# Launch order, pooling means on ScalarE, two row buffers for thirteen pairs of weight sums, and channel tiles added ahead of their sums

## What is computed

```python
    c_act = jax.nn.silu(c)
    mod = (c_act @ w_ada[l] + b_ada[l])[:, None, :]
    u = layer_norm(x) * (1 + sc_m) + sh_m
    z = u @ w_in[l]
    y_pool = pool_mixer(z_pool, w_pool[l], pool_scale[l]) @ w_br_pool[l]
    y_attn = chunk_attention(z_q, z_k, z_v, rel_bias[l]) @ w_br_attn[l]
    y_conv = conv_module(z_conv, conv_w[l], conv_b[l], conv_ln_g[l], conv_ln_b[l]) @ w_br_conv[l]
    merged = gates[:, :, 0] * y_pool + gates[:, :, 1] * y_attn + gates[:, :, 2] * y_conv
    x = layer_norm(ALPHA * x + g_m * (merged @ w_o[l]), ln_mix_g[l], ln_mix_b[l])
    h = jnp.square(jax.nn.relu(u @ w_ff1[l] + b_ff1[l]))        # u from the new x
    x = layer_norm(ALPHA * x + g_f * (h @ w_ff2[l] + b_ff2[l]), ln_ff_g[l], ln_ff_b[l])
```

## Time and profile before

| what | value |
|---|---|
| median of 3 runs | 1504.99 us (1504.74 to 1505.49) |
| the profiled execution | 1508.53 us, span 1506.4 us |
| TensorE busy | 1445.0 us, 96% |
| VectorE busy | 980.5 us, 65% |
| ScalarE busy | 586.4 us, 39% |
| GpSimd busy | 474.5 us, 31% |
| mean granted clock of TensorE | 0.992 of full speed |

### The profile page before, as it was taken

How to read it: one execution, slowest core, us unless ns; L and a number is a source line. 1 busy time by engine, 2 the same in 40 slices (tenths; PEclk the granted TensorE clock), 3 DMA queues, 4 the chain that set the end, 5 groups by cost and what they waited for, 6 DMA issues and landing times.

```text
span 1506.4 us, 17601 instructions
## 1 busy us (share of the span) xinstructions
PE 1445.0 (96%) x6802; PEld 1203.4 (80%) x6802; DVE 980.5 (65%) x1244; ACT 586.4 (39%) x824; POOL 474.5 (31%) x385
## 2 busy tenths in 40 slices
PE   7799899999899999997999999999999999999998
PEld 7687688878778888886888887788888888888886
DVE  3878697878867445432376879766565644675494
ACT  3311254544554111110252766444444544433351
POOL 1007500000000788996202534344344311240021
PEclk9999999999999999998999999999999999999999
DMA  9774110000102667766362264444443869656371
GB/s 351 239 252 128 41 30 23 29 28 23 29 1 62 225 236 267 270 252 214 119 215 92 84 234 157 140 154 154 154 154 133 277 233 362 225 182 230 120 236 57
DMA packets 149124, 241.51 MB, mean 160 GB/s; under 512 B 9464, under 2 KB 79278, under 8 KB 147000
## 3 DMA queue, kind: packets, MB, share of 16 engines
q1 hardware_dynamic: 134824, 177.04, 35.2%
q0 software_dynamic: 14224, 63.45, 11.3%
HBM read 170.17 MB, written 70.29 MB: 160 GB/s over the span
## 4 chain that ended last, share of the span: by engine, by line
PE 67%; DVE 11%; DMA 8%; POOL 7%; issue 3%; ACT 3%; SPq 0%; DVEq 0%; ACTq 0%; POOLq 0%
PE ps L1878 19%; PE ps L1880 18%; PE ps L1879 18%; PE ps L1979 7%; DMA tw_scratch<-tw_sum 6%; PE ps L1898 2%; POOL tw_sum L780 2%; POOL tw_rows L781 1%; PE ps L2037 1%; DVE partial L1341 1%; POOL tw_sum L783 1%; POOL tw_sum L778 1%; DVE bn L1308 1%; DVE mid L1624 1%; DVE mid L1427 1%
## 5 line engine op out<-in xcount | busy, mean ns | idle before, releaser
L1878 PE MATMUL ps<-act_hi,w_hi 128*128 128x512 f32 (+1 forms) x512 | 199.9, 390 | 9.4 <-DVE w_lo L1498 8.8
L1879 PE MATMUL ps<-act_lo,w_hi 128*128 128x512 f32 (+1 forms) x512 | 196.9, 385 | 0.0
L1880 PE MATMUL ps<-act_hi,w_lo 128*128 128x512 f32 (+1 forms) x512 | 196.8, 384 | 0.0
L1745 DVE TENSOR_TENSOR part_lo<-k_raw,part_hi 128x1024 fp32r<-128x1024 f32 x112 | 154.2, 1414 | 49.0 <-ACT part_hi L866 46.7
L1878 PE MATMUL ps<-part_hi 128*128 128x512 f32 x448 | 174.3, 389 | 0.0
L1879 PE MATMUL ps<-part_lo,part_hi 128*128 128x512 f32 x448 | 174.3, 389 | 0.0
L1880 PE MATMUL ps<-part_hi,part_lo 128*128 128x512 f32 x448 | 174.3, 389 | 0.0
L866 ACT ACTIVATE part_hi<-k_raw 128x1024 fp32r<-128x1024 f32 x112 | 116.3, 1059 | 110.2 <-DMA k_raw<-tw_scratch 84.3
L1498 DVE TENSOR_TENSOR w_lo<-w_raw,w_hi 128x1024 fp32r<-128x1024 f32 x30 | 63.7, 2122 | 116.3 <-ACT w_hi L866 116.3
L1878 PEld LDWEIGHTS ps<-act_hi,w_hi 128*128 128x128 f32 x512 | 97.0, 189 | 30.1 <-DVE w_lo L1498 9.7
L1879 PEld LDWEIGHTS ps<-act_lo,w_hi 128*128 128x128 f32 x512 | 97.0, 190 | 19.1 <-issue 0.7
(11 more groups left out here) (250 smaller groups left out, 3403.9 us busy)
## 6 DMA issues: line engine op xcount, KB each, us to landing
k_raw<-h_scratch SPq DMA_DIRECT2D x112, 256.0 KB, 4.0
k_raw<-tw_scratch SPq DMA_DIRECT2D x112, 256.0 KB, 5.3
ada<-in_w_ada_dram SPq DMA_DIRECT2D x11, 2048.0 KB, 10.1
w_raw<-in_w_in_dram SPq DMA_DIRECT2D x42, 512.0 KB, 5.2
tw_rows<-in_w_ff_dram POOLq DMA_DIRECT2D x16, 1024.0 KB, 5.5
tw_scratch<-tw_rows POOLq DMA_DIRECT2D x16, 1024.0 KB, 4.3
h_scratch<-h_sum POOLq DMA_DIRECT2D x64, 256.0 KB, 3.2
pair_raw<-in_w_ff_dram SPq DMA_DIRECT2D x13, 1024.0 KB, 6.0
```

The source lines that it names most:

```text
L1745: nc.vector.tensor_tensor(part_lo[s][:, :, :], k_raw[rs][:, :, :], f(part_hi[s][:, :, :]), ALU.subtract)\
L1878: nc.tensor.matmul(out, sh, mh, start=first, stop=False)
L1879: nc.tensor.matmul(out, sh, ml, start=False, stop=False)
L1880: return nc.tensor.matmul(out, sl, mh, start=False, stop=last)
```

## The change

- Launch: TensorE transposes the small rows between the two direct chunks; VectorE cuts block 1 behind the `mod` columns; SP issues the load of chunk 4 ahead of its wait for `rel_done`.
- Pooling: ScalarE does the scaling of columns 16 and up (`scale_means`), for tile 0 behind its cut of block 7, for tile 1 at attention step 2; GpSimd waits for it and then subtracts. `zero_q(1)` comes before tile 1's sums and not after them.
- Weight sums: `TWO_ROWS` goes from 15 to 13. Pairs 13, 14 and 15 use `tw_rows[0]` alone, and VectorE's wait ahead of tiles 5 and 6 is for 12 stored pairs and not 14.
- Channel sums: VectorE adds the two channel tiles (into `conv_sum`) and the two squares (into `sq[:, 0]`), and TensorE sums one tile instead of two.
- Some semaphores are merged (`rel_stored` and `gate_stored` into `scratch_stored`, `c_sig_done` and `c_act_done` into `c_done`), `pooled_done` counts to 4 instead of 2. These lines are left out below.

```diff
@@ -43,7 +43,7 @@
 AHEAD = 6
-TWO_ROWS = 15
+TWO_ROWS = 13
 FIRST_NORM = 88
...
@@ -53,6 +53,7 @@
 MIX_STEP = 24
+MEANS_STEP = 2
 
...
@@ -113,6 +114,7 @@
     conv_std = conv_sig[1]
+    conv_sum = conv_sig[0]
 
...
@@ -458,9 +459,9 @@
                 sp.dma_start(t[:, :], b_ada[0:1, col:col + D].partition_broadcast(P)).then_inc(ada_bias_in, 16)
+            load_ada(4)
             sp.wait_ge(rel_done, 1)
-            sp.dma_start(rel_dram, rel_ext[:, :]).then_inc(rel_stored, 16)
-            load_ada(4)
+            sp.dma_start(rel_dram, rel_ext[:, :]).then_inc(scratch_stored, 16)
             for n in range(2, 9):
...
@@ -705,20 +706,18 @@
-            def window_mean(c, half, total):
-
-                rows = slice(64 * half, 64 * half + 64)
-                first = total[rows, 0:16]
-                link(nc.gpsimd.tensor_tensor(first, first, inv_count[rows, c, :], ALU.mult))
-                link(nc.gpsimd.tensor_scalar(total[rows, 16:SEQ], total[rows, 16:SEQ], inv_count[rows, c, 15:16], None,
-                                             ALU.mult))
-                z = z_pool[rows, c, :]
-                ins = nc.gpsimd.tensor_tensor(z, total[rows, :], z, ALU.subtract)
-                if half == 1:
-                    ins.then_inc(pooled_done, 1)
-                    pool.wait_ge(pooled_done, c + 1)
-                else:
-                    link(ins)
+            def window_means(c, totals):
+
+                halves = [slice(0, 64), slice(64, P)]
+                for rows, total in zip(halves, totals):
+                    first = total[rows, 0:16]
+                    nc.gpsimd.tensor_tensor(first, first, inv_count[rows, c, :], ALU.mult).then_inc(means_summed, 1)
+                pool.wait_ge(means_summed, 2 * c + 2)
+                pool.wait_ge(means_scaled, 2 * c + 2)
+                for rows, total in zip(halves, totals):
+                    z = z_pool[rows, c, :]
+                    nc.gpsimd.tensor_tensor(z, total[rows, :], z, ALU.subtract).then_inc(pooled_done, 1)
+                pool.wait_ge(pooled_done, 2 * c + 2)
 
...
@@ -734,21 +733,19 @@
             shifted_sum(b, a, 2, slice(64, P))
-            window_mean(0, 0, a)
-            window_mean(0, 1, b)
+            window_means(0, (a, b))
             pool.wait_ge(partial_done, 10 - N_DIRECT)
             zero_q(0)
             pool.wait_ge(zp_done, 2)
+            pool.wait_ge(partial_done, 12 - N_DIRECT)
+            zero_q(1)
             z = z_pool[:, 1, :]
             shifted_sum(a, z, 1)
             shifted_sum(b, a, 2)
             shifted_sum(a, b, 4)
             shifted_sum(b, a, 8, slice(64, P))
-            window_mean(1, 0, a)
-            window_mean(1, 1, b)
-            pool.wait_ge(partial_done, 12 - N_DIRECT)
-            zero_q(1)
-            pool.wait_ge(gate_stored, 32)
+            window_means(1, (a, b))
+            pool.wait_ge(scratch_stored, 48)
             nc.gpsimd.memset(w_pool_bd[:, :, :], 0.0).then_inc(consts_done, 1)
...
@@ -915,6 +912,15 @@
                 cut_hi(n + 2)
+
+            def scale_means(c):
+                act.wait_ge(means_summed, 2 * c + 2)
+                for half in range(2):
+                    rows = slice(64 * half, 64 * half + 64)
+                    total = mid[rows, 3 + half, 16:SEQ]
+                    copy(total, total, scale=inv_count[rows, c, 15:16]).then_inc(means_scaled, 1)
+
+            scale_means(0)
 
...
@@ -1011,6 +1017,8 @@
                     take_half(*half_of(pair, i))
+                if a == MEANS_STEP:
+                    scale_means(1)
 
...
@@ -1368,9 +1376,9 @@
             cut_lo(0)
-            cut_lo(1)
             dve.wait_ge(reduced, 4)
             mod_columns(0, 6)
+            cut_lo(1)
             for k in range(KT):
...
@@ -1457,6 +1465,9 @@
                     conv_tap(a)
+                elif a == 2 * TAPS:
+                    dve.wait_ge(tap_done, 2 * TAPS)
+                    nc.vector.tensor_tensor(conv_sum[:, :], mid[:, 6, :], mid[:, 7, :], ALU.add).then_inc(tap_done, 1)
                 if a < N_STEPS:
...
@@ -1484,6 +1495,8 @@
                                                op0=ALU.mult, op1=ALU.add).then_inc(centred, 1)
+            dve.wait_ge(squared, 2)
+            nc.vector.tensor_tensor(sq[:, 0, :], sq[:, 0, :], sq[:, 1, :], ALU.add).then_inc(squared, 1)
             cut_branch_lo(0)
...
@@ -1917,12 +1930,12 @@
-            pe.wait_ge(c_act_done, 1)
+            pe.wait_ge(c_done, 2)
             direct_chunk(0)
-            direct_chunk(1)
             pe.wait_ge(small_in, 16 * 8)
             nc.tensor.transpose(ps[:, 4, 0:ROWS_A], rows_a[:, :], ident[0:ROWS_A, 0:ROWS_A]).then_inc(cols_t, 1)
             nc.tensor.transpose(ps[:, 5, 0:ROWS_C], rows_c[:, :], ident[0:ROWS_C, 0:ROWS_C]).then_inc(cols_t, 1)
+            direct_chunk(1)
             reduce_chunk(2)
...
@@ -2075,9 +2088,7 @@
                 for h in range(2):
-                    for t in range(2):
-                        ins = nc.tensor.matmul(ps[:, bank + h, :], ones_row[:, :], src[:, t, half_cols(h)],
-                                               start=t == 0, stop=t == 1)
+                    ins = nc.tensor.matmul(ps[:, bank + h, :], ones_row[:, :], src[:, half_cols(h)], start=True, stop=True)
                 return ins
...
@@ -2102,8 +2113,8 @@
                     pe.wait_ge(biased, N_STEPS)
-                    pe.wait_ge(tap_done, 2 * TAPS)
-                    conv_sums(4, mid[:, 6:8, :]).then_inc(csum_done, 1)
+                    pe.wait_ge(tap_done, 2 * TAPS + 1)
+                    conv_sums(4, conv_sum).then_inc(csum_done, 1)
                 between(a, 0)
...
@@ -2117,9 +2128,9 @@
                     gate_half(2, 0)
-            pe.wait_ge(squared, 2)
+            pe.wait_ge(squared, 3)
             pe.wait_ge(centred, 2)
-            conv_sums(4, sq).then_inc(csum_done, 1)
+            conv_sums(4, sq[:, 0, :]).then_inc(csum_done, 1)
             gate_half(2, 1).then_inc(g_done, 1)
```

More of the change, by code:

```diff
@@ L253, in trunk_layer @@
         pool_step, dve_step = sem("pool_step"), sem("dve_step")
-        c_sig_done, c_act_done, cols_t, cols_done, rel_done = (
-            sem("c_sig_done"), sem("c_act_done"), sem("cols_t"), sem("cols_done"), sem("rel_done"))
+        c_done, cols_t, cols_done, rel_done = sem("c_done"), sem("cols_t"), sem("cols_done"), sem("rel_done")
         partial_done, reduced, mod_done, gates_done = (
@@ L274, in trunk_layer @@
         pv_done, o_copied = sem("pv_done"), sem("o_copied")
-        q_zeroed, conv_w_done, gate_stored, gate_in = (
-            sem("q_zeroed"), sem("conv_w_done"), sem("gate_stored"), sem("gate_in"))
+        q_zeroed, conv_w_done, gate_in = sem("q_zeroed"), sem("conv_w_done"), sem("gate_in")
+        means_summed, means_scaled = sem("means_summed"), sem("means_scaled")
         pm_done, pm_scaled, tap_done = sem("pm_done"), sem("pm_scaled"), sem("tap_done")
@@ L474, in load_bias @@
                     sp.dma_start(bias_rev[pair % 2][h * CHUNK:(h + 1) * CHUNK, :], src).then_inc(bias_in[pair % 2], 16)
-            sp.wait_ge(rel_stored, 16)
+            sp.wait_ge(scratch_stored, 16)
             load_bias(0)
@@ L540, in _ @@
             sp.dma_start(plain_raw[:, :], wff1_view[:, :, 2 * P:3 * P]).then_inc(row_in[0], 16)
-            sp.wait_ge(gate_stored, 32)
+            sp.wait_ge(scratch_stored, 48)
             for i, t in enumerate((gate_mix, gate_ff)):
@@ L886, in _ @@
             act.wait_ge(c_in, 16)
-            nc.scalar.activation(c_sig[:, :], c_raw[:, :], ACT.Sigmoid).then_inc(c_sig_done, 1)
+            nc.scalar.activation(c_sig[:, :], c_raw[:, :], ACT.Sigmoid).then_inc(c_done, 1)
             for i in range(ST + 1):
@@ L958, in take_v @@
                 else:
-                    act.wait_ge(rel_stored, 16)
+                    act.wait_ge(scratch_stored, 16)
                 if pair >= 2:
@@ L985, in _ @@
                     if tile == ST:
-                        act.wait_ge(pooled_done, 2)
+                        act.wait_ge(pooled_done, 4)
                     ts = slice(tile % ST * P, (tile % ST + 1) * P)
@@ L1319, in scale_bias @@
                     .then_inc(norm_ready, 1)
-            dve.wait_ge(c_sig_done, 1)
-            nc.vector.tensor_tensor(c_act[:, :], c_raw[:, :], c_sig[:, :], ALU.mult).then_inc(c_act_done, 1)
-            dve.wait_ge(c_act_done, 1)
+            dve.wait_ge(c_done, 1)
+            nc.vector.tensor_tensor(c_act[:, :], c_raw[:, :], c_sig[:, :], ALU.mult).then_inc(c_done, 1)
+            dve.wait_ge(c_done, 2)
             for i in range(ST):
@@ L2067, in mix_pool @@
                     pe.wait_ge(vt_free, 2 * (MIX_STEP // STEPS + 1))
-                    pe.wait_ge(pooled_done, 2)
+                    pe.wait_ge(pooled_done, 4)
                     pe.wait_ge(pool_w_in, 64)
```

4 lines of the change are left out of this document (2 added, 2 removed).

## The result

| | before | after |
|---|---|---|
| median | 1505.15 us (1503.31 to 1507.72, 8 runs) | 1509.59 us (1507.97 to 1510.62, 8 runs) |
| ratio, 95% interval | | 1.0028 (1.0019 to 1.0037) |
| profiled execution, span | 1508.53, 1506.4 us | 1509.3, 1507.5 us |
| granted clock, mean | 0.992 | 0.988 |

The change is slower by 0.28%, 6.9 us above the forecast of 1502.7 and 0.6 us above the range. The difference of the profiled executions was forecast at -2.3 us and came out at +0.8. All ratios here are of fast executions; one of experiment 5, which took 2053 us at a granted clock of 0.66, is left out of its ratio.

What follows compares the result with a forecast made beforehand. TensorE is busy nearly all the time, so only its standing or slow-clock places count. -6.8 - 4.3 - 3.3 + 12.1 = -2.3 us gives 1506.2 profiled, 1502.7 us median; 8-in-10 range 1497 to 1509.

Steps and rivals of the forecast that it cites:

- Launch, -6.8: At the launch, transposes between the direct chunks let VectorE start sooner; `mod` written at 46.9 instead of 53.71, -6.8 us.
- Pooling, -4.3: Before attention, chunk 11 runs alone and TensorE's wait for `k_lo` goes, -6.8 us, less costs in attention: -4.3 us.
- What it keeps for channel tile 0 ends when it did: GpSimd's remaining pooling work for tile 0 was to end at its old time despite waiting for ScalarE's scaling.
- an earlier 1.3 us wait shrinks by 1.0: A TensorE wait before the `k_lo` one was to shrink by 1.0 us, counted within pooling's -6.8 us.
- The price in steps 3 to 5: In attention, tile 1's two subtractions slow VectorE by 2.2 us, plus 0.3 for ScalarE's scaling.
- The fourth case: Rival: the two subtractions hold VectorE their whole 4.8 us, pooling brings -1.7, total 1505.3 us; chance 0.20.
- Channel sums, -3.3: At both pairs of channel sums TensorE's eight records fall to four, -1.7 us twice, -3.3 us.
- Weight sums, +12.1: Tile 5's stall goes, but three serial pair steps of 22.9 us make TensorE stand 20.6 us at the last tile.
- I take the difference to stay: The profiled execution's 3.5 us above the median of 1505.0 us was assumed to hold for the changed kernel too.
- The rival on the slower side: Serial tail at SP's wait for `tw_stored`: steps of 25.6 us cost +20.2, total 1510.8 us; slower beyond 24.7; chance 0.13.

Runs made afterwards that it cites:

- experiment 5: The changed kernel with GpSimd's two subtractions for tile 0 moved behind chunk 11's sum; 1507.09 us, ratio 1.0009 to the kernel before.
- Experiment 1: The kernel before, unchanged, timed and traced once more; 1506.76 us, ratio 0.9999, profiled execution 1504.46 us.

## Why the prediction was wrong

- **Launch, -6.8.** Right in its mechanism: `mod` is 7.8 us earlier, chunk 4 7.0 us in the trace, and the median gains 5.7.
- **Pooling, -4.3: the step that failed.** "What it keeps for channel tile 0 ends when it did" is nearly so (135.1, where 134.5 is the old end less launch's 7.0 us), but the prediction drew from it that "an earlier 1.3 us wait shrinks by 1.0". It didn't ask where the two subtractions stand on the way to that end. GpSimd waits 8.13 us for ScalarE, so the subtraction that cost chunk 9 time which it could spare moves onto chunk 10, which TensorE waits for. Chunk 10's seven steps take 9.53 us instead of 7.56, and the wait grows to 1.9. Up to attention that is -4.0 us instead of -6.8; experiment 5 gives back 3.5 by moving the subtractions, which shows the cause. The price in steps 3 to 5 was right: +2.9 (31.6 - 28.7) against 2.5. In the trace the part is -1.1 us where -4.3 was forecast, and alone by the medians +1.4 (0 to +2.7). The 2.5 us between these two stay open.
- **The fourth case**, that the subtractions hold VectorE for as long as they last, had the right mechanism and too high a price. At chunk 10 each subtraction draws out one step, which ends 0.5 us behind it; each costs VectorE 2.03 us, where they last 2.4 and 2.7. That is 4.05 of 5.20 us at chunk 10, and in attention it is 2.9 of 5.29. The operations with two inputs in SBUF suffer and the one that reads PSUM doesn't, which agrees with what the Trainium skill says (GPSIMD Engine Reference, Key points). The `tensor_scalar` suffers as well; no row shows whether it ran in a two-port mode.
- **Channel sums, -3.3.** 1.88 us twice instead of 3.59, in the trace a lead that grows from 8.2 us at step 8 to 11.5 at the first load of the weight sums, and -4.8 us (-6.5 to -3.0) by the medians: right.
- **Weight sums, +12.1.** Right in each step: serial steps of 24.95, 23.13 and 21.59 us (667.18 to 736.85), 23.2 in the mean against 22.9, TensorE standing 20.9 against 20.6, the part +11.8. The first step has GpSimd's multiplication drawn out to 6.47 us, and the last, with TensorE idle, is the shortest. It is below the prediction's lower bound of 21.9, which the rows don't give either: a load of 5.5, a store of 5.6 and the 11.5 us between them make 22.6.
- **"I take the difference to stay": the second step that failed.** The changed kernel's profiled execution lies at its median (1509.3, 1509.6), where that of before lay 3.5 us above. By traces the miss of 6.9 us is 3.1 us of the sum (3.2 of it pooling) and 3.8 of this. With the 3.1 alone the time would have been 1505.8, inside the range. Experiment 1 puts most of the excess into the stall at tile 5, which the change removes. But the thirteen pairs alone cost the median 11.8 us and not 15.5, which speaks against that account, and later medians of the kernel before (1505.8 to 1507.1) leave less of an excess than the 1505.0 of three runs. By medians the miss is pooling's 5.7 us, launch's 1.1, less 1.5 of the channel sums and 0.3 of the weight sums, and 1.9 within the error of four runs. So pooling is 3.2 of the 6.9 us by the traces and 5.7 by the medians, and how much this step is worth beside it stays open.
- **The rival on the slower side** had the right place and the wrong price: no step reached 24.7 us but the first. The change is slower with serial steps as forecast, because the gain beside them was smaller.

## What to carry to other kernels

Before a wait is made longer, list what stands behind it in the same queue: here 20.9 us of standing came from three loads that needed nothing of it, and moving them ahead gave 1.1% back. When an engine hands half of its work to another and waits for it, its remaining instructions move together and later; look up which work they then stand beside, since a chunk with slack and the next without it look the same in a busy share. Ask for the shortest and the longest of a group before its mean is used as a price: 1.39 us was the mean of operations of 0.75 to 2.75. Where the profiled execution lies off the median, find the stretch that holds the difference before it is carried over to a kernel without that stretch.

## What was not expected of the hardware

- A memset of GpSimd (64x1024) doesn't slow VectorE's `scalar_tensor_tensor` of 128x512: seven took 9.55 us beside two subtractions alone and 9.53 beside the same two and four memsets. A subtraction costs about 2.0 us, all of it in one step, which takes 2.78 us instead of 0.75.
- VectorE's `tensor_scalar` beside a GpSimd instruction mostly ends just behind it, even behind a memset: 2.26 instead of 0.35, 2.21 instead of 0.28 us beside subtractions, 1.25 instead of 0.48 beside a memset. One case is otherwise: in the kernel before one of 1.25 us (136.41) ends 1.4 us ahead of the GpSimd multiplication beside it (134.75 to 139.08).
- In seven profiled executions with fifteen pairs VectorE's wait at the merge of tile 5 was either 11.9 us (three) or 17.8 to 18.8 us (four), and nothing between. What chooses was not found.
